# A two-layer hybrid block with a 16384-expert feed-forward: twelve expert blocks beside the key search in three fp32r passes, low parts by GpSimd, key numbers out of packed words

## The reference, cut to what matters

```python
def peer_ffn(x, w_query, sub_keys, down, up):
    q = (xt @ w_query).reshape(T, H, 2, PEER_HALF)
    s = jnp.einsum('thcd,cnd->thcn', q, sub_keys)
    sv, si = lax.top_k(s, K)                                   # the 16 best of 128, for each half
    cand_s = (sv[:, :, 0, :, None] + sv[:, :, 1, None, :]).reshape(T, H, K * K)
    cand_i = (si[:, :, 0, :, None] * PEER_NKEYS + si[:, :, 1, None, :]).reshape(T, H, K * K)
    top_s, pos = lax.top_k(cand_s, K)                          # the 16 best pairs
    idx = jnp.take_along_axis(cand_i, pos, axis=-1)
    gate = jax.nn.softmax(top_s, axis=-1)
    a = jnp.einsum('thkd,td->thk', down[ib], xb)
    c = gb * jax.nn.gelu(a)
    return jnp.einsum('thk,thkd->td', c, up[ib])
```

## Time and profile before

| what | value |
|---|---|
| median of 3 runs | 2927.83 us (2926.03 to 2928.36) |
| the profiled execution | 2924.12 us, its span 2921.9 us |
| PE busy, of the span | 2891.7 us, 99% |
| DVE busy | 2013.2 us, 69% |
| ACT busy | 1466.4 us, 50% |
| POOL busy | 17.0 us, 1% |
| TensorE clock granted, mean | 0.999 |
| DMA | 530.08 MB, mean 181 GB/s |

### The profile page before, as it was taken

How to read it: one execution, slowest core, us unless ns; L and a number is a source line. 1 busy time by engine, 2 the same in 40 slices (tenths; PEclk the granted TensorE clock), 3 DMA queues, 4 the chain that set the end, 5 groups by cost and what they waited for, 6 DMA issues and landing times.

```text
span 2921.9 us, 43689 instructions
## 1 busy us (share of the span) xinstructions
PE 2891.7 (99%) x17162; PEld 2559.0 (88%) x17162; DVE 2013.2 (69%) x3105; ACT 1466.4 (50%) x2295; POOL 17.0 (1%) x41
## 2 busy tenths in 40 slices
PE   8999999999999999999999999999999999999998
PEld 7888887889999898888788999987899988888997
DVE  7878998665555687999876555566656556565554
ACT  6622774544444563177455444445455445554443
POOL 0000000000000000000000000000000000000000
PEclk9999999999999999999999999999999999999999
DMA  6344556765554534444677555456555656554564
GB/s 217 110 160 148 171 180 207 272 247 191 182 184 175 170 114 146 156 166 171 211 259 260 180 194 200 172 179 179 183 164 183 186 189 182 172 180 138 155 187 134
DMA packets 223373, 530.08 MB, mean 181 GB/s; under 512 B 13514, under 2 KB 87408, under 8 KB 211952
## 3 DMA queue, kind: packets, MB, share of 16 engines
q1 hardware_dynamic: 221872, 521.11, 54.0%
q0 software_dynamic: 1344, 6.82, 0.6%
HBM read 507.81 MB, written 20.06 MB: 181 GB/s over the span
## 4 chain that ended last, share of the span: by engine, by line
PE 96%; DVE 2%; ACT 1%; DMA 0%; issue 0%; SPq 0%; DVEq 0%; ACTq 0%
PE ps L2452 16%; PE ps L1344 15%; PE ps L2436 13%; PE ps L1394 12%; PE ps L1404 12%; PE ps L1378 12%; PE ps L574 4%; PE ps L565 3%; PE ps L1333 2%; PE ps L2696 2%; PE ps L1136 1%; PE ps L698 1%; PE ps L2619 0%; PE ps L2603 0%; PE ps L1319 0%; DVE ring_lo L548 0%
## 5 line engine op out<-in xcount | busy, mean ns | idle before, releaser
L2090 DVE TENSOR_TENSOR ring_lo<-ring,w_hi 128x1024 fp32r<-128x1024 f32 x320 | 388.7, 1224 | 263.7 <-ACT w_hi L2086 262.2
L2086 ACT ACTIVATE w_hi<-ring 128x1024 fp32r<-128x1024 f32 x320 | 336.5, 1057 | 262.6 <-PE ps L2452 178.3
L1344 PE MATMUL ps<-h_t,ring 128*128 128x256 f32 x2048 | 463.5, 379 | 0.9 <-ACT arena L957 0.9
L1344 PEld LDWEIGHTS ps<-h_t,ring 128*128 128x128 f32 x2048 | 379.1, 190 | 47.5 <-issue 1.3
L1394 PE MATMUL ps<-h_t_lo,down_hi 128*128 128x256 f32 x1024 | 288.2, 281 | 0.0
L1394 PE MATMUL ps<-h_t_expert,down_lo 128*128 128x256 f32 x1024 | 287.8, 281 | 0.0
L1394 PE MATMUL ps<-h_t_expert,down_hi 128*128 128x256 f32 x1024 | 286.8, 280 | 0.0
L2436 PE MATMUL ps<-h_t_hi,w_hi 128*128 128x256 f32 x928 | 260.1, 280 | 2.8 <-ACT arena L2242 2.7
L2436 PE MATMUL ps<-h_t_lo,w_hi 128*128 128x256 f32 x928 | 261.5, 282 | 0.0
L2436 PE MATMUL ps<-h_t_hi,ring_lo 128*128 128x256 f32 x928 | 259.6, 280 | 0.0
L1883 DVE TENSOR_TENSOR up_lo<-ring,up_hi 128x2048 fp32r<-128x2048 f32 x64 | 146.7, 2293 | 97.4 <-ACT up_hi L1020 97.4
(11 more groups left out here) (478 smaller groups left out, 6612.8 us busy)
## 6 DMA issues: line engine op xcount, KB each, us to landing
ring<-in_peer_down SPq DMA_DIRECT2D x128, 1024.0 KB, 5.1
ring<-in_w_in SPq DMA_DIRECT2D x140, 512.0 KB, 3.7
ring<-in_peer_up SPq DMA_DIRECT2D x68, 1024.0 KB, 4.9
ring<-in_w SPq DMA_DIRECT2D x132, 512.0 KB, 3.7
ring<-in_peer_up SPq DMA_DIRECT2D x120, 512.0 KB, 4.2
arena<-late_gates SPq DMA_DIRECT2D x16, 1024.0 KB, 7.3
ring<-in_w_out SPq DMA_DIRECT2D x16, 512.0 KB, 3.7
ring<-in_peer_w_query SPq DMA_DIRECT2D x16, 512.0 KB, 4.2
```

What stands on the lines that cost most here:

```text
L1344: m = pe.e.matmul(PS[:, act_bank(b), j * T:(j + 1) * T], RING[:, b % 2, j * D + kc * P:j * D + (kc + 1) * P], HT[:, kc, :], start=kc == 0, ...
L2086: a.e.activation(W_HI[:, g % HI_SLOTS, :], RAW[:, g % RAW_SLOTS, :], ACT.Copy).then_inc(*a.count(f"c{g}_hi"))
L2090: v.e.tensor_tensor(RAW_LO[:, g % RAW_SLOTS, :], RAW[:, g % RAW_SLOTS, :], W_HI[:, g % HI_SLOTS, :].bitcast(F32), ALU.subtract).then_inc(* ...
```

## The change

- Blocks 1 to 12 are split into high and low parts. ACT copies each half of a block to one of five slots of `out_lo`/`out_hi` (`lead_high`), one block ahead of its own gelu. POOL subtracts (`lead_low`) into `ring_lo`. PE runs 3 x 16 fp32r matmuls of 128x256 for each block (`act_passes`). Block 0 stays f32.
- The tokens are split once: ACT copies `h_t` to `h_t_expert`, DVE subtracts into `h_t_hi`, before `top_keys`.
- The weights of the first 13 blocks rotate through four places of the ring instead of two (`LEAD_PLACE`). The first two `up` blocks are loaded after block 14's `down`.
- In `top_keys` the 16 key numbers of a half (7 bits each) are packed into four words of 32 bits, with two xor tables (six small instructions). The choice then is bitwise: masks from the place's bits select the word, and a shift selects the byte. ACT's table copies and all predicated copies go.

```diff
+LEAD_SPLIT = [1, 2, 3, 4, 5, 6, 7, 8, 9, 10, 11, 12]
+LEAD_POOL = [1, 2, 3, 4, 5, 6, 7, 8, 9, 10, 11, 12]
+LEAD_PLACE = [(b // 2 % 2, b % 2) if b < LEAD else (b % 2, 0) for b in range(HELD + 2)]
+LEAD_SLOTS = 5
...
+        packed, at = [], 0
+        for n in (8, 8, 4, 2, 2):
+            packed.append(split(EQ[:, at:at + HC * n].bitcast(U32), "p (c w) -> p c w", w=n))
+            at += HC * n
+        ODD, PAIR, WORD, ACROSS, WITHIN = packed
+        CHOSEN = split(EQ[:, at:at + 6 * 2 * P].bitcast(U32), "p (n c k) -> p n c k", n=6, c=2)
...
+        def lead_slot(b, j):
+            n = (2 * LEAD_SPLIT.index(b) + j) % LEAD_SLOTS
+            return (OUT_LO[:, n, :] if n < OUT_SLOTS else OUT_HI[:, n - OUT_SLOTS + 1, :])
+        def lead_slot_free(b, j):
+            n = 2 * LEAD_SPLIT.index(b) + j - LEAD_SLOTS
+            return f"act_half{LEAD_SPLIT[n // 2]}{n % 2}" if n >= 0 else "h11_mm"
+        def lead_raw(b, j, of):
+            slot, part = LEAD_PLACE[b]
+            return of[:, 4 * slot + 2 * part + j, :]
+        def lead_high(a, b):
+            a.e.wait_ge(*a.at(f"down_in{b}"))
+            for j in range(2):
+                a.e.wait_ge(*a.at(lead_slot_free(b, j)))
+                a.e.activation(lead_slot(b, j), lead_raw(b, j, RAW), ACT.Copy).then_inc(*a.count(f"lead_hi{b}{j}"))
+        def lead_low(e, b):
+            for j in range(2):
+                e.e.wait_ge(*e.at(f"lead_hi{b}{j}"))
+                e.e.tensor_tensor(lead_raw(b, j, RAW_LO), lead_raw(b, j, RAW), lead_slot(b, j).bitcast(F32), ALU.subtract) \
+                    .then_inc(*e.count(f"lead_lo{b}{j}"))
...
+                for b in LEAD_POOL:
+                    lead_low(p, b)
...
+            a.e.wait_ge(*a.at("ht"))
+            a.e.wait_ge(*a.at("h11_mm"))
+            a.e.activation(HT_EXPERT[:, :, :], HT[:, :, :], ACT.Copy).then_inc(*a.count("lead_ht_hi"))
...
+            lead_high(a, LEAD_SPLIT[0])
             for b in range(LEAD):
+                if b in LEAD_SPLIT and b != LEAD_SPLIT[-1]:
+                    lead_high(a, LEAD_SPLIT[LEAD_SPLIT.index(b) + 1])
                 act_out(b)
-                if b in (2, 8):
-                    t = int(b == 8)
-                    a.e.wait_ge(*a.at(f"key_numbers{t}"))
-                    for c in range(2):
-                        half = HALF_KEYS[:, c, :, :].rearrange("p (h k) i -> p h k i", h=PEER_HEADS)
-                        a.e.activation(half, TOPF.rearrange("p (h c) k -> p h c k", c=2)[:, :, c, 0::2].unsqueeze(2).broadcast_to(
-                            [P, PEER_HEADS, TOPK, TOPK // 2]), ACT.Copy).then_inc(*a.count(f"half_keys{t}" if c else None))
...
+            def act_passes(b):
+                pe.e.wait_ge(*pe.at("key_ev0" if b < 2 else f"act_ev{b - 2}"))
+                for j in range(2):
+                    pe.e.wait_ge(*pe.at(f"lead_lo{b}{j}"))
+                    hi, lo = lead_slot(b, j), lead_raw(b, j, RAW_LO)
+                    for kc in range(KD):
+                        o = slice(kc * P, (kc + 1) * P)
+                        for n, (w, x) in enumerate(((hi, HT_EXPERT), (hi, HT_HI), (lo, HT_EXPERT))):
+                            m = pe.e.matmul(PS[:, act_bank(b), j * T:(j + 1) * T], w[:, o], x[:, kc, :],
+                                            start=kc == 0 and n == 0, stop=kc == KD - 1 and n == 2)
+                    m.then_inc(*pe.count(f"act_half{b}{j}"))
+                pe.mark(f"act_mm{b}")
             for b in range(LEAD):
-                for q in range(4):
-                    act_quarter(b, q)
+                if b in LEAD_SPLIT:
+                    if b == LEAD_SPLIT[0]:
+                        pe.e.wait_ge(*pe.at("lead_ht_lo"))
+                    act_passes(b)
+                else:
+                    for q in range(4):
+                        act_quarter(b, q)
...
+            v.e.wait_ge(*v.at("lead_ht_hi"))
+            v.e.tensor_tensor(HT_HI[:, :, :], HT[:, :, :], HT_EXPERT[:, :, :].bitcast(F32), ALU.subtract) \
+                .then_inc(*v.count("lead_ht_lo"))
...
-            v.e.tensor_copy(TOPF, TOPI).then_inc(*v.count(f"key_numbers{t}"))
+            v.e.tensor_scalar(ODD, TOPI[:, :, 1::2], 8, None, ALU.logical_shift_left).then_inc(*v.count())
...
+            v.e.wait_ge(*v.mine(len(REACH)))
+            v.e.tensor_tensor(PAIR, ODD, TOPI[:, :, 0::2], ALU.bitwise_or).then_inc(*v.count())
+            v.e.wait_ge(*v.mine())
+            v.e.tensor_scalar(ODD[:, :, 0:4], PAIR[:, :, 1::2], 16, None, ALU.logical_shift_left).then_inc(*v.count())
+            v.e.wait_ge(*v.mine())
+            v.e.tensor_tensor(WORD, ODD[:, :, 0:4], PAIR[:, :, 0::2], ALU.bitwise_or).then_inc(*v.count())
+            v.e.wait_ge(*v.mine())
+            v.e.tensor_tensor(ACROSS, WORD[:, :, 0:2], WORD[:, :, 2:4], ALU.bitwise_xor).then_inc(*v.count())
+            v.e.tensor_tensor(WITHIN[:, :, 0:1], WORD[:, :, 0:1], WORD[:, :, 1:2], ALU.bitwise_xor).then_inc(*v.count())
+            v.e.wait_ge(*v.mine(1))
+            v.e.tensor_tensor(WITHIN[:, :, 1:2], ACROSS[:, :, 0:1], ACROSS[:, :, 1:2], ALU.bitwise_xor).then_inc(*v.count())
...
+            def table(words, n):
+                return words.rearrange("p (h c) w -> p c h w", c=2)[:, :, :, n].unsqueeze(3).broadcast_to([P, 2, PEER_HEADS, TOPK])
...
+            FOURTH, THIRD, LOW_BITS, LEFT, RIGHT, KEPT = (CHOSEN[:, n, :, :] for n in range(6))
...
-            for n in range(4):
-                v.e.tensor_scalar(CHOICE[:, n, :, :], KI, 1 << n, None, ALU.bitwise_and).then_inc(*v.count())
-            v.e.wait_ge(*v.at(f"half_keys{t}"))
-            v.e.wait_ge(*v.mine())
-            v.e.tensor_copy(LB[:, 14:15], COMMON[:, 0:1]).then_inc(*v.count())
-            for c in range(2):
-                v.e.copy_predicated(
-                    HALF_KEYS[:, c, :, :].rearrange("p (h k) i -> p h k i", h=PEER_HEADS),
-                    CHOICE[:, 0, c, :].rearrange("p (h k) -> p h k", h=PEER_HEADS).unsqueeze(3).broadcast_to(
-                        [P, PEER_HEADS, TOPK, TOPK // 2]),
-                    topf[:, :, c, 1::2].unsqueeze(2).broadcast_to([P, PEER_HEADS, TOPK, TOPK // 2])).then_inc(*v.count())
-            for n, w in ((1, 4), (2, 2)):
-                step = TOPK // 2 // w
-                v.e.wait_ge(*v.mine())
-                v.e.tensor_copy(LB[:, 14:15], COMMON[:, 0:1]).then_inc(*v.count())
-                for c in range(2):
-                    v.e.copy_predicated(HALF_KEYS[:, c, :, 0::step],
-                                        CHOICE[:, n, c, :].unsqueeze(2).broadcast_to([P, P, w]),
-                                        HALF_KEYS[:, c, :, step // 2::step]).then_inc(*v.count())
-            v.e.wait_ge(*v.mine())
-            v.e.tensor_copy(HKR[:, t, 0:2, :], HALF_KEYS[:, :, :, 0]).then_inc(*v.count())
-            v.e.wait_ge(*v.mine())
-            v.e.tensor_copy(LB[:, 14:15], COMMON[:, 0:1]).then_inc(*v.count())
-            for c in range(2):
-                v.e.copy_predicated(HKR[:, t, c, :], CHOICE[:, 3, c, :], HALF_KEYS[:, c, :, 4]).then_inc(*v.count())
+            v.e.tensor_scalar(FOURTH.bitcast(I32), KI.bitcast(I32), 28, 31, ALU.logical_shift_left, ALU.arith_shift_right) \
+                .then_inc(*v.count())
+            v.e.tensor_scalar(THIRD.bitcast(I32), KI.bitcast(I32), 29, 31, ALU.logical_shift_left, ALU.arith_shift_right) \
+                .then_inc(*v.count())
+            v.e.tensor_scalar(LOW_BITS, KI, 3, 3, ALU.bitwise_and, ALU.logical_shift_left).then_inc(*v.count())
+            v.e.wait_ge(*v.mine(2))
+            v.e.tensor_tensor(ranked(LEFT), ranked(FOURTH), table(ACROSS, 0), ALU.bitwise_and).then_inc(*v.count())
+            v.e.tensor_tensor(ranked(RIGHT), ranked(FOURTH), table(WITHIN, 1), ALU.bitwise_and).then_inc(*v.count())
+            v.e.wait_ge(*v.mine(1))
+            v.e.tensor_tensor(ranked(LEFT), ranked(LEFT), table(WORD, 0), ALU.bitwise_xor).then_inc(*v.count())
+            v.e.wait_ge(*v.mine(1))
+            v.e.tensor_tensor(ranked(RIGHT), ranked(RIGHT), table(WITHIN, 0), ALU.bitwise_xor).then_inc(*v.count())
+            v.e.wait_ge(*v.mine())
+            v.e.tensor_tensor(RIGHT, RIGHT, THIRD, ALU.bitwise_and).then_inc(*v.count())
+            v.e.wait_ge(*v.mine())
+            v.e.tensor_tensor(KEPT, LEFT, RIGHT, ALU.bitwise_xor).then_inc(*v.count())
+            v.e.wait_ge(*v.mine())
+            v.e.tensor_tensor(KEPT, KEPT, LOW_BITS, ALU.logical_shift_right).then_inc(*v.count())
+            v.e.wait_ge(*v.mine())
+            v.e.tensor_scalar(KEPT, KEPT, NKEYS - 1, None, ALU.bitwise_and).then_inc(*v.count())
+            v.e.wait_ge(*v.mine())
+            v.e.tensor_copy(HKR[:, t, 0:2, :], KEPT).then_inc(*v.count())
...
-                for b in range(2):
-                    sp.e.wait_ge(*sp.at(f"h{n - 2 + b}_mm"))
-                    peer_block(sp, "down", b, b, l, f"down_in{b}")
-                    peer_block(sp, "up", b, b, l, f"up_in{b}")
-
-                for b in range(2, HELD + 2):
```

(33 more changed lines are left out.)

## The result

The changed kernel takes 2956.68 us (median of 4 runs, 2954.71 to 2959.94) against 2928.1 before: a ratio of 1.0099, 95% interval 1.0086 to 1.0113, or 28.6 us slower. The forecast was 44 slower (2972, range 2898 to 3000). The profiled execution took 2956.14 us, its span is 2954.3.

The account below looks back on a forecast made before the run. PE's f32 blocks bound the stage, with DVE close behind; under POOL's lock, 2 x (20.1 for late search results + 2 for PE's clock) = +44 us, giving 2968 profiled, 2972 on the median, range 2898 to 3000.

Parts of the forecast that it names:

- The sign and the mechanism: Slower by 44 us, as POOL's subtractions lock out DVE instructions with two SBUF operands or in a fast form; chance 0.60.
- Rival 1: DVE beside POOL: no lock when POOL runs first, or a short one; 2901 us; chance 0.28.
- Rival 2: DVE wins and POOL gets no turn, so PE stalls for low parts: +3 a layer, 2934 at most; chance 0.06.
- The covers: Before the search, ACT's token split (1.9 us) and DVE's subtraction (2.29 us) fit idle time; loads also keep up.
- Rival 3: Every DVE instruction is held by POOL, MAX8 included: DVE loses 52.8 us a layer, time 3011; chance 0.06.
- Rival 4: POOL above 2.83 us a subtraction sets the pace; three passes bring PE nothing; inside the forecast's 0.60.
- walk: DVE's search followed step by step under the lock, at 2.2 us a subtraction: 20.1 us late in each layer.
- the late `hkr`: DVE's search result, which PE's transposes need, comes at 295.4 instead of 275.3: +20.1 us a layer.
- PE's clock: After PE's 35 us wait its clock may be low: between 0 and 5 us a layer, taken as 2.
- DVE advances at 0.22 of its pace: While low parts are made, POOL holds the lock 4.4 of every 5.66 us, 78%, leaving DVE 0.22.
- B: DVE's shift, packing steps and candidate sums in each token half: 2.5 us alone, 11.3 under the lock.
- D and E: DVE's places and choice in each token half: 8.4 us of work, ending at 256.4 in the first half.

Follow-up runs that it names:

- e3b: Changed kernel with POOL subtracting one element of each half block instead of 1024, and PE's third pass rereading the high part: 2898.51 us, ratio 0.9897.
- e4: Changed kernel with POOL writing zeros over each half block (memset) instead of subtracting: 2902.02 us (one run).
- e7: Changed kernel with all 24 subtractions, the intermediate arrays of places and choice alternating between PSUM and SBUF: 2919.18 us, ratio 0.9963.

## Why the prediction was right, and where its size was off

The sign and the mechanism held. The range, 2898 to 3000, reached over rivals 1 and 2 as well, so that lying in it says little; the sign and the traces decide. PE's blocks take 5.69 us (I said 5.66) and its 13 blocks end at 262.8, where the sum, with the stage's later start, gives 262.2. DVE's undisturbed half takes 37.2 us (37.8). The covers held: ACT's split of the tokens, DVE's subtraction, the loads. Rival 1, no lock in this order, is refuted by L2077 and by e3b. Rival 3, every DVE instruction held, is refuted by the MAX8 and search groups at their usual pace. Rival 2, POOL starving, is refuted by POOL's 2.44 to 2.54 us in the middle of a contested stretch, 0.1 above its 2.40 (2.59 at most). Rival 4 did not come about: a pair of subtractions takes 4.7 of PE's 5.69 us.

POOL's subtraction was priced at 2.2 us and took 2.40, or 2.36 from start to start in a pair; the estimate from the figure of the Trainium skill (GPSIMD Engine Reference, § 3.1), 2.25, was nearer. That error made the forecast smaller: with the measured price the same walk gives an estimated 22 us a layer instead of 20.1, so by luck it cancelled a part of the two errors below. The rule of the Trainium skill (SBUF — State Buffer, § Who interferes with whom) is now shown here in both orders, for two-operand and for fast-form instructions, and for POOL writing only (e4).

The sum said +20.1 us a layer for the late `hkr` and +2 for PE's clock; measured are 14.2 and 0.4. Two terms were off.

- The step "DVE advances at 0.22 of its pace" was too low, for B above all. The walk had B take 11.3 us; it took 6.5 (206.75 to 213.2), as its four sums fell into the 0.9 us in which POOL waits for ACT. D and E together took 32 us for some 8.1 us of work, 0.25, and ended before the last subtractions. I had treated the hold as a share of time that falls evenly on every instruction. In the trace it is a turn: one DVE instruction stands behind one subtraction, and in each gap as many run as fit. Thirteen instructions were held for nearly a whole subtraction, 2.1 to 2.2 us each, and one (L2064) for 0.5: 28.3 us for the first half, where the walk had 33.5. The other eleven of the 24 subtractions met searches or gaps and held nothing for long.
- PE's clock after its rest was the right worry and cost next to nothing. While PE was idle the granted clock fell to 0.50, the 1.2 GHz level, and PE's work resumed at it. These windows (columns as above) show 0.50 and 0.55 from the transposes at 291.56 to 295.00, and 1.00 from there on:

```profile
285.00:290.00 5.00, 0.00 (x0) 0.00 (x0) 4.70 (x15) 0.10 (x1) 0.00 (x0) 0.50 0.00 0
290.00:292.50 2.50, 0.94 (x5) 0.97 (x6) 1.27 (x6) 0.00 (x0) 0.00 (x0) 0.50 0.00 0
292.50:295.00 2.50, 2.50 (x9) 2.11 (x8) 2.50 (x7) 0.00 (x0) 0.00 (x0) 0.55 0.00 0
295.00:297.00 2.00, 2.00 (x11) 1.77 (x10) 1.97 (x3) 0.68 (x3) 0.00 (x0) 1.00 0.00 0
```

The transposes took 1.51 us instead of 0.82, and the 12 f32 matmuls that cover the one-hot preparation (24 records) took 6.27 instead of 5.35, but before PE had waited 0.97 us for the one-hot matrices behind them, and now it did not. The first gate sums start 7.35 us after the transposes instead of 6.97: 0.4 us a layer, where I had put 2.

The walk is 5.9 us a layer too long (20.1 against 14.2; 5.2 of them are the hold, most of the rest the length of an undisturbed half, 37.2 instead of 37.8), and the clock 1.6. Twice the two are 15.0 of the 15.4 us between forecast and measurement. The own range of the forecast mixed its bases: its lower end, 2945, stands on the profiled execution and its upper, 3008, on the median.

## What to carry to other kernels

Before work goes to an idle GpSimd, list what VectorE does at that time. An instruction with two SBUF operands, or a cast or scalar operation from SBUF to SBUF in the fast form, waits until the GpSimd instruction that is running has ended, here up to 2.2 us behind a subtraction of 2.4. Searches and maxima with one operand do not wait, and neither do two-operand instructions with one operand in PSUM. So count the instructions that will meet one, and not the share of time in which GpSimd is busy. If the work must overlap, move one of VectorE's operands to PSUM, or put GpSimd's instructions beside the one-operand stretches.

## What the runs showed of the hardware that I had not expected

- A DVE operand in PSUM takes an instruction out of the contest at almost no cost: 0.29 us for 128x128 and 0.42 for 128x256 beside a running subtraction (e7), the same as with both in SBUF alone. The integer shifts, ands and xors work there too; only casts and scalar operations lose their fast form (0.42 us for 128x256, where SBUF to SBUF takes 0.29).
- Read and write sides differ. A GpSimd memset of 0.96 us let two-operand instructions pass at 0.28 us and held only casts and a scalar operation from SBUF to SBUF; the longest took 1.01 us (e4).
- The two engines took turns at instruction boundaries: in the contested stretches of the changed kernel a subtraction was delayed by one short DVE instruction (2.44 to 2.59 us instead of 2.40), and a DVE instruction by one subtraction, also where the next subtraction could have followed at once.
